# Weight buffers of a split-precision transformer kernel, spaced 32 bytes apart in SBUF

## The reference, cut to what matters

```python
z = h @ w_in                                              # attn_project: 2048 -> 4864 columns
return (y * jax.nn.silu(gate)) @ w_out                    # gated_out
u, gate = jnp.split(h @ w_in, 2, axis=-1)                 # fourier_mixer: 2048 -> 8192
proj = jnp.einsum("bsd,dp->bsp", n, w_in)                 # token_mixer
up = depthwise_conv_centered(jnp.einsum("bsd,df->bsf", n, w_ffn_in), conv_ffn_w)   # 2048 -> 11264
return jnp.einsum("bsf,fd->bsd", jax.nn.silu(gate) * val, w_ffn_out)               # 5632 -> 2048
```

## Time and profile before

| | |
|---|---|
| median of 3 runs | 2885.03 us |
| the 3 runs | 2883.73, 2885.03, 2910.47 us |
| the profiled execution | 2913.37 us, of which the span is 2911.6 us |
| TensorE busy | 96% of the span |
| weight loads busy | 91% |
| DVE, ACT, POOL busy | 62%, 43%, 9% |
| mean granted clock of TensorE | 0.981 of full speed |
| moved by transfers | 546.84 MB, mean 188 GB/s |

### The profile page before, as it was taken

The page is one execution under the profiler, slowest core; times in us unless marked ns, Lnnn a source line. Parts: engine busy times, 40 slices in busy tenths (PEclk is TensorE's granted clock), DMA queues, the critical chain, the costliest instruction groups (busy, mean ns, idle before and its releaser), DMA issues.

```text
span 2911.6 us, 50366 instructions
## 1 busy us (share of the span) xinstructions
PE 2786.7 (96%) x22070; PEld 2638.8 (91%) x22070; DVE 1809.9 (62%) x2229; ACT 1246.7 (43%) x1375; POOL 270.2 (9%) x330
## 2 busy tenths in 40 slices
PE   6899999998999999989999999989999999999998
PEld 3598877797988998989999999979999999999998
DVE  2358767688777545566556555795666665466653
ACT  4323444345443334444434448453544443344444
POOL 0022002120111000003113110021000000000000
PEclk9899999998999999999999999999999999999999
DMA  9867535574776554435555544430445555555553
GB/s 368 325 226 247 194 133 201 202 277 149 251 247 225 192 199 162 169 136 190 174 173 175 174 167 146 154 139 1 145 160 188 189 181 188 189 184 187 183 185 138
DMA packets 93034, 546.84 MB, mean 188 GB/s; under 512 B 12656, under 2 KB 12816, under 8 KB 47888
## 3 DMA queue, kind: packets, MB, share of 16 engines
q1 hardware_dynamic: 69552, 466.39, 45.3%
q0 software_dynamic: 20480, 67.13, 6.8%
q10 hardware_dynamic: 2784, 10.11, 0.9%
HBM read 541.48 MB, written 2.10 MB: 187 GB/s over the span
## 4 chain that ended last, share of the span: by engine, by line
PE 67%; DVE 6%; ACT 2%; issue 2%; DMA 1%; DVEq 0%; ACTq 0%
PE bank L727 67%; DVE r L2156 2%; DVE f L2727 1%; ACT r L1459 1%; PE bank L787 1%; DVE f L2193 0%; DMA f<-in_later 0%; DVE f L2791 0%; ACT f L1821 0%; DVE f L2788 0%; DVE f L2804 0%; DVE f L2780 0%; DVE f L2539 0%; DMA f<-in_units 0%; DVE f L2556 0%
## 5 line engine op out<-in xcount | busy, mean ns | idle before, releaser
L727 PE MATMUL bank<-r,r 128*128 128x256 f32 (+1 forms) x19596 | 2444.1, 287 | 44.8 <-DVE r L2156 20.5
L727 PEld LDWEIGHTS bank<-r,r 128*128 128x128 f32 x19596 | 2376.2, 190 | 100.8 <-DVE r L2156 28.2
L2156 DVE TENSOR_TENSOR r<-f,r 128x2048 fp32r<-128x2048 f32 (+2 forms) x447 | 961.1, 2151 | 724.4 <-ACT r L1459 723.1
L1459 ACT CAST r<-f 128x2048 fp32r<-128x2048 f32 (+2 forms) x447 | 792.7, 1775 | 886.4 <-PE bank L727 684.2
L727 PE MATMUL bank<-f,f 128*128 128x128 f32 (+10 forms) x1992 | 326.5, 375 | 58.2 <-DMA f<-in_units 23.1
L727 PEld LDWEIGHTS bank<-f,f 128*128 128x128 f32 (+3 forms) x1992 | 218.8, 177 | 121.7 <-issue 53.1
L2193 DVE SCALAR_TENSOR_TENSOR f<-f,f,f 128x512 f32<-128x512 f32 x240 | 179.8, 749 | 53.8 <-DMA f<-in_later 38.2
L3052 POOL DMA_DIRECT2D f<-in_later x256 | 137.5, 537 | 799.8 <-DVE f L2193 475.8
L2727 DVE SCALAR_TENSOR_TENSOR f<-f,f,f 128x255 f32<-128x255 f32 (+1 forms) x272 | 132.9, 491 | 8.8
L1476 ACT COPY f<-bank 128x512 f32<-128x512 f32 x149 | 83.9, 584 | 115.6 <-PE bank L727 109.3
L3061 POOL TENSOR_TENSOR f<-f,f 32x512 f32<-32x512 f32 x24 | 62.7, 2614 | 658.4 <-DVE f L2665 658.4
(11 more groups left out here) (235 smaller groups left out, 925.2 us busy)
## 6 DMA issues: line engine op xcount, KB each, us to landing
f<-in_units SPq DMA_DIRECT2D x346, 1024.0 KB, 4.8
f<-in_units SPq DMA_DIRECT2D x124, 768.0 KB, 4.3
f<-in_later POOLq DMA_DIRECT2D x256, 256.0 KB, 4.3
f<-in_units SPq DMA_DIRECT2D x8, 576.0 KB, 4.4
f<-in_x ACTq DMA_DIRECT2D x2, 1024.0 KB, 12.8
f<-in_ctx ACTq DMA_DIRECT2D x2, 1024.0 KB, 12.2
f<-in_x_turned ACTq DMA_DIRECT2D x1, 2048.0 KB, 13.4
out<-f SPq DMA_DIRECT2D x4, 256.0 KB, 3.7
```

What stands on the lines that cost most here:

```text
L727: return e.matmul(o, lhsT, rhs, start=start, stop=stop, skip_group_check=True)
L1459: e.copy(unit_view(high[HIGH_OF[u]][1], u), unit_view(raw[RAW_OF[u]][0], u)).then_inc(*up("w_hi", ("hi", u)))
L2156: e.tensor_tensor(unit_view(raw[RAW_OF[u]][1], u), unit_view(raw[RAW_OF[u]][0], u), unit_view(high[HIGH_OF[u]][1], u).bitcast(F32), ALU.su ...
```

## The change

Behind each of W's seven buffers 8 floats (32 bytes) are left free. W grows by 32 floats (128 bytes), so K and R start 32 floats later. No instruction is added, removed or moved, and no size or wait changes.

```diff
+STAGGER = 8
...
-        W = Region(0, UNIT * (SLOTS + HIGH) + 32)
-        raw = [W.place(UNIT) for _ in range(SLOTS)]
-        high = [W.place(UNIT) for _ in range(HIGH)]
+        W = Region(0, UNIT * (SLOTS + HIGH) + 64)
+        raw, high = [], []
+        for i in range(SLOTS + HIGH):
+            (raw if i < SLOTS else high).append(W.place(UNIT))
+            W.at += STAGGER
         K = Region(W.size, KEEP)
         R = Region(W.size + KEEP, SLAB - KEEP - W.size)
```

## The result

The change took 2933.49 us in the median of 4 runs (2931.81 to 2933.9), against 2887.92 us before (4 runs, 2883.73 to 2910.47). The ratio is 1.0141, with a 95% interval of 1.0087 to 1.0194. The kernel became slower, by 1.4% and by 45.6 us between the medians. The prediction was 2938 us.

The account below looks back on a forecast made before the run. TensorE was taken to bound the kernel, by matmul count times start spacing. From the profiled 2913.4 us, + 28.8 us gave 2942, or 2934 with - 8.5 us; the middle was 2938 us, overall range 2865 to 2950.

Parts of the forecast that it names:

- What bounds the kernel: Whole span: TensorE busy 96%, line 727 67%; time is matmul count times start spacing, plus stages the change leaves unaltered.
- tight: Dense stretches of line 727 with matmul starts 113.1 ns apart, against about 117.6 ns in those called loose.
- Spacing is a phase of two streams, and the last stage explains the two groups of runs.: Weight loads and running matmuls lock into either spacing; from 2072 us on this is worth 31 us between runs.
- ACT, DVE and transfers cost nothing.: Cast 1911 ns and subtraction 2290 ns stay covered by units of 5.4 us; transfers stay hidden at DMA share 0.53 to 0.66.
- The four cases with another relation: Units whose weights lie at 0, 160 or 320 bytes relative to activations, not 192: spacings 117.0 to 118.0 ns.
- The rival that addresses do not matter: Only pauses set the spacing of line 727's products: 2885 us, or 2911 with a loose last stretch; chance 0.22.
- The tight phase needs the relation 192, which only high 0 keeps, and always next to low weights that have lost it.: Linear layers: of seven buffers six leave 192 bytes, so all 6,400 products at 113.1 ns go to 117.6.
- The sum: Linear layers' products: 2913.4 + 28.8 = 2942 us, or 2934 us with 8.5 us less; middle 2938 us.
- the first term: Linear layers: 6,400 products go from 113.1 to 117.6 ns, + 28.8 us.
- The term of - 8.5 us: Linear layers: all 17,100 products lose 0.5 ns if they go to the 117.1 ns that `wq` shows.
- The upper bound: Linear layers' products at the 118.9 ns of `dv`: 22 us more than all loose, 2964 us.
- Runs no longer in two groups.: Whole kernel after the change: runs should no longer lie in two groups 26 us apart.

Follow-up runs that it names:

- bare products: Own kernel without the reference's computation, only triples of products at chosen start addresses, 48 to a unit with a pause before each; its spacing differs by address.
- the shift of 256 bytes: Kernel before with W enlarged by 96 floats in place of the change's 32, no gaps, moving K and R by 256 bytes: 2888.12 us, ratio 0.9988.
- the first map: Own kernel issuing only products: ten units at each of 16 address relations, one at each of 256 high and low weight pairs; spacings up to 124.0 ns.
- the second map: Products-only kernel, low activations also moved by 0 to 448 bytes against the high ones, 128 cases of four units: nine tight in all four, none below 113.3 ns.
- the worst placement: Against the kernel before, no gaps within the raw or high buffers, all raw ones placed at relation 384 and all high ones at 96: 2987.91 us, ratio 1.0289.

## Why the prediction was right

*What bounds the kernel.* Borne out for most of the span. The instructions are the same, but "plus stages that the change does not alter" left out that TensorE waits in some stages, and there a wider spacing only shortens the waits. Of the 50 units from `qb1` up to `fg` 27 were tight before and 3 are after, yet `fg` begins no later (the first row is before, the second after):

```profile
695.94 4.37 PE L727 MATMUL bank<-r,r 128*128 128x256 f32 x17 [3.46 <-issue]
695.06 5.22 PE L730 MATMUL bank<-r,r 128*128 128x256 f32 x21 [3.46 <-issue]
```

*Spacing is a phase of two streams, and the last stage explains the two groups of runs.* That there are two phases is borne out by the bare products and by the shift of 256 bytes, where the last stage is tight at an unchanged instruction stream. That it explains the two groups is likely but not shown. That the load and the running matmul are in each other's way fits bare products whose spacing depends on addresses alone, but which reads collide, and what happens inside SBUF or TensorE, no run shows.

*ACT, DVE and transfers cost nothing.* Borne out for the change: 1907 and 2290 ns, no more idle time ahead of the matmuls, and a DMA share of 0.53 in the long stretches.

*The four cases with another relation mean that they are loose.* The conclusion held, and it was the step with the least behind it. The rival that addresses do not matter was given 0.22, and the first map rules it out.

*"The tight phase needs the relation 192, which only high 0 keeps, and always next to low weights that have lost it."* Half wrong. The high weights need 192 or 448 for a reliable tight phase, but low weights at 320 do not spoil it. They secure it: that pair is tight in 28 of 28 units, where 192 with 192 can be either. So 1,270 products stayed tight. The mistake came from `wq`, where both weights had 320 to the high queries and the low queries lay at 192. I took it for a verdict on 320 as such, without its place in the triple. In the second map that case (320, 320, moved by 384) is loose in all four units.

*The sum.* Expected from the profiled execution of before: + 28.8 us for all loose, less 8.5 us if they go to what `wq` shows, so + 20 to + 29. Measured between the two profiled executions: 2931.8 - 2913.4 = + 18.4 us. I added up the spacings of all units in both traces, which hold all 19,560 fp32r products of the units. They grew by 28.6 us, as much as the first term. Two errors of opposite sign had cancelled: 1,270 products stayed tight, which is 5.7 us less, and the others came to 118.2 ns in the mean where loose units had 117.8, some 6 us more. The term of - 8.5 us did not come. The two units of `wq` that it rests on gave 117.1 ns, but all eight come to 117.4 already before. In its place 10 us of the growth were lost in waits, about 8 us of them before 696 us and 2 to 3 us between 1786 and 2147 us. So 2938 for 2933.5 is good in the mechanism and partly luck in the number.

*The upper bound.* The 118.9 ns for `dv` divide a window of 29 us by a count that takes in matmuls at its ends. One merged row gives (25.44 - 0.28) / 209 = 120.4 ns:

```profile
1359.75 25.44 PE L727 MATMUL bank<-r,r 128*128 128x256 f32 x210
```

All products at that spacing would have given some 2990 us, not 2964. Nor was it a bound: a unit of the change reaches 122.3 ns, and the worst placement 124.6.

*Runs no longer in two groups.* Borne out: 2.1 us from the lowest to the highest.

## What to carry to other kernels

When dense matmuls on identical shapes show two mean durations in one trace (here 276 and 281 ns), look at the start addresses of the stationary and the moving operands modulo 256 bytes before looking at any schedule. For a stream of weight load and matmul pairs in which several operands alternate, sweep the relations in a small kernel and place the buffers at one that is tight after every pause; here that is worth 2% against the staggered placement and 0.5% against the one before. A stagger that gives each buffer another relation is the opposite of that: it averages over many of them. And a tighter spacing pays only in stages where TensorE does not wait for something else.

## What was not expected of the hardware

Thirty-two bytes of address change the pace of TensorE, at a granted clock of 1.00. With 128-column loads and 256-column fp32r matmuls the spacing lies between 113.3 and 124.6 ns. At some relations there are two stable phases, which can change after a pause and are then held, in the last stage for thousands of products. With everything else equal, that is worth 6,843 x 4.5 = 31 us there by the estimate of the prediction, about the distance of the two groups of runs.
